# Gate and up of the experts with the hi and lo halves of 64 tokens in one stationary block of 128 columns

## What is computed

```python
def run_block(args):
    tok, g, e = args
    xb = x2[tok]
    hb = jax.nn.silu(xb @ w_gate[e]) * (xb @ w_up[e])
    return (hb @ w_down[e]) * g[:, None].astype(x2.dtype)
```

## Time and profile before

| | |
|---|---|
| median of 3 runs | 2676.31 us (2673.6 to 2676.85) |
| span of the profiled execution | 2682.0 us |
| expert loop, from the first gather to the last subtraction | about 603 to 1222 us |
| PE, DVE, ACT busy over the span | 2241.3, 1577.4, 1063.9 us |
| mean granted clock of TensorE | 0.872 |

### The profile page before, as it was taken

One profiled execution on the slowest core, in us unless ns is written; L12 is line 12 of the kernel. 1 busy time (PEld: TensorE's weight loads), 2 busy tenths in 40 slices (PEclk: granted clock), 3 DMA queues, 4 the chain that ended last, 5 costly groups with the idle time before them and its releaser, 6 DMA issues. The chain is left out here.

```text
span 2682.0 us, 27601 instructions
## 1 busy us (share of the span) xinstructions
PE 2241.3 (84%) x10272; PEld 1841.8 (69%) x10272; DVE 1577.4 (59%) x1629; ACT 1063.9 (40%) x1243; POOL 433.0 (16%) x310
## 2 busy tenths in 40 slices
PE   6998966757999999992897787886488986899997
PEld 5885655656777787772776677765467865688786
DVE  4114578356788788884249999999733244333312
ACT  3224531215677676773243324433343222322211
POOL 0002121001111111110134454343300011000000
PEclk9996557858999999996798988888689998899999
DMA  4210000407999999984232222222023221333321
GB/s 144 73 48 1 1 0 1 167 32 248 324 342 361 333 356 365 357 316 145 51 95 78 64 63 79 79 63 64 0 89 84 94 94 32 87 95 96 107 79 63
DMA packets 251273, 346.55 MB, mean 129 GB/s; under 512 B 13951, under 2 KB 149623, under 8 KB 250151
## 3 DMA queue, kind: packets, MB, share of 16 engines
q1 hardware_dynamic: 240432, 332.49, 37.3%
q0 software_dynamic: 5200, 8.40, 1.0%
q10 hardware_dynamic: 5543, 4.34, 0.5%
HBM read 341.19 MB, written 12.65 MB: 132 GB/s over the span
## 5 line engine op out<-in xcount | busy, mean ns | idle before, releaser
L1335 DVE TENSOR_TENSOR wlo_e<-raw_e,whi_e 128x2048 fp32r<-128x2048 f32 x192 | 432.1, 2292 | 83.6 <-ACT whi_e L1269 83.6
L47 PE MATMUL pall<-hT_hi,w_lo 128*128 128x512 f32 x864 | 354.7, 411 | 53.2 <-DVE yT L2181 33.6
L1646 ACT CAST w_hi<-w_raw 128x2048 fp32r<-128x2048 f32 x89 | 169.5, 1904 | 540.9 <-PE pall L49 540.9
L1654 DVE TENSOR_TENSOR w_lo<-w_raw,w_hi 128x2048 fp32r<-128x2048 f32 x75 | 171.8, 2291 | 352.6 <-ACT w_hi L1646 352.6
L1269 ACT CAST whi_e<-raw_e 128x2048 fp32r<-128x2048 f32 x192 | 357.2, 1914 | 0.0
L48 PE MATMUL pall<-hT_lo,w_hi 128*128 128x512 f32 x864 | 348.1, 403 | 0.0
L49 PE MATMUL pall<-hT_hi,w_hi 128*128 128x512 f32 x864 | 346.5, 401 | 0.0
L2193 DVE SCALAR_TENSOR_TENSOR mixed<-yT,cols,mixed 128x512 f32<-128x512 f32 x240 | 251.2, 1047 | 7.6
L47 PEld LDWEIGHTS pall<-hT_hi,w_lo 128*128 128x128 f32 x864 | 170.4, 197 | 93.5 <-DVE yT L2181 36.4
L47 PE MATMUL pall<-whi_e,xT_lo 128*128 128x512 f32 x512 | 204.6, 400 | 9.6 <-DVE wlo_e L1335 9.6
L49 PE MATMUL pall<-whi_e,xT_hi 128*128 128x512 f32 x512 | 201.2, 393 | 0.0
(11 more groups left out here) (443 smaller groups left out, 4440.0 us busy)
## 6 DMA issues: line engine op xcount, KB each, us to landing
raw_e<-in_w_expert_up_dram SPq DMA_DIRECT2D x64, 1024.0 KB, 8.2
raw_e<-in_w_expert_down_dram SPq DMA_DIRECT2D x64, 1024.0 KB, 7.6
raw_e<-in_w_expert_gate_dram SPq DMA_DIRECT2D x64, 1024.0 KB, 7.1
w_raw<-in_w_in_dram SPq DMA_DIRECT2D x80, 512.0 KB, 5.4
w_raw<-in_w_gate_up_dram SPq DMA_DIRECT2D x44, 512.0 KB, 5.1
w_raw<-in_w_down_dram SPq DMA_DIRECT2D x22, 512.0 KB, 3.9
mixed<-in_w_in_dram SPq DMA_DIRECT2D x10, 1024.0 KB, 5.0
A<-acs_rows SPq DMA_DIRECT2D x8, 1024.0 KB, 4.9
```

The source lines that it names most:

```text
L47: nc.tensor.matmul(out, w_lo, m_hi, start=start, stop=False)
L1335: ins = nc.vector.tensor_tensor(wlo[j][:, :], raw[j][:, :], whi[j][:, :].bitcast(F32), ALU.subtract)
L1646: self.nc.scalar.copy(self.hi[i][:, :], self.raw[i][:, :]).then_inc(self.s_hi, 1)
L1654: (engine or self.nc.vector).tensor_tensor(self.lo[i][:, :], self.raw[i][:, :], self.hi[i][:, :].bitcast(F32), ALU.subtract).then_inc(self ...
```

## The change

Gate and up of one expert take two matmuls per k-block in place of three. The transposed tokens are kept in one tile `xs` of [128, 8, 128], hi of the 64 tokens in columns 0 to 63 and lo in columns 64 to 127. One matmul with all 128 columns stationary and the hi weights moving gives hi x hi in output rows 0 to 63 and lo x hi in rows 64 to 127; a second, with the 64 hi columns stationary and the lo weights moving, adds hi x lo to rows 0 to 63. The two halves are added when the result is turned: `gate_sb` and `up_sb`, copies of the banks in SBUF, are the stationary operands of fp32 matmuls (`combine`) whose moving operand is `st2`, two 64 x 64 identities on top of each other. So silu and the product with up are done in turned form, on 256 columns (`sgT`, `hidT`), and `h_turn` falls away. `y_out` is one copy of 64 x 1024 on ScalarE, one turn later. The loops are unrolled in Python.

```diff
+        xs = sb("xs", [P, KD, 2 * SLOTS], F32R)
+        st2 = sb("st2", [P, SLOTS])
...
             def project(e, out, j0):
                 for j in (j0, j0 + 1):
-                    pe.wait_ge(s["lo"], e * U + j + 1 if not (isinstance(e, int) and e == 0 and j == 3) else U)
+                    pe.wait_ge(s["lo"], made(e, j))
                     for k in range(4):
                         kk = 4 * (j % 2) + k
-                        last = split_mm(nc, out, xT_hi[:, kk, :], xT_lo[:, kk, :], k4(whi[j])[:, k, :], k4(wlo[j])[:, k, :],
-                                        kk == 0, kk == KD - 1)
...
+                        mm(out, xs[:, kk, :], k4(whi[j])[:, k, :], start=kk == 0, stop=False, skip_group_check=True)
+                        last = mm(out[0:SLOTS, :], xs[:, kk, 0:SLOTS], k4(wlo[j])[:, k, :], start=False, stop=kk == KD - 1,
+                                  skip_group_check=True)
...
+            def combine(e):
+
+                pe.wait_ge(s["gate"], e + 1)
+                pe.wait_ge(s["up"], e + 1)
+                if e >= 1:
+                    pe.wait_ge(s["sg"], e)
+                    pe.wait_ge(s["hid"], e)
+                for out, t in ((GT, gate_sb), (UT, up_sb)):
+                    for k in range(4):
+                        last = mm(out[:, k * SLOTS:k * SLOTS + SLOTS], t[:, k * P:k * P + P], st2[:, :], start=True, stop=True)
+                last.then_inc(s["comb"], 1)
...
+            for e in range(E):
+                pe.wait_ge(s["xlo"], e + 1)
+                if e >= 1:
+                    pe.wait_ge(s["gate"], e)
                 project(e, GATE, 0)
-                if not first:
-                    h_turn(e - 1)
+                if e >= 1:
+                    combine(e - 1)
+                    pe.wait_ge(s["up"], e)
                 project(e, UP, 2)
...
+                if e + 1 < E:
+                    x_turn(e + 1)
+                if e >= 1:
+                    down(e - 1)
+            combine(E - 1)
+            down(E - 1)
```

ScalarE's new steps and its order, and VectorE's:

```diff
+            def gate_out(e):
+                act.wait_ge(s["used"], used(e, 1))
+                if e >= 1:
+                    act.wait_ge(s["comb"], e)
+                nc.scalar.copy(gate_sb[:, :], GATE).then_inc(s["gate"], 1)
...
             def silu(e):
-                act.wait_ge(s["used"], e * U + 2)
-                if not isinstance(e, int) or e >= 1:
+                act.wait_ge(s["comb"], e + 1)
+                if e >= 1:
                     act.wait_ge(s["hid"], e)
-                nc.scalar.activation(sg[:, :], GATE, ACT.Silu).then_inc(s["sg"], 1)
+                nc.scalar.activation(sgT[:, :], GT, ACT.Silu).then_inc(s["sg"], 1)
...
+            for e in range(E):
+                hi(e, 3)
+                if e >= 2:
+                    y_out(e - 2)
+                if e >= 1:
+                    hi(e - 1, 4)
+                gate_out(e)
+                if e >= 1:
+                    hi(e - 1, 5)
+                    silu(e - 1)
+                if e + 1 < E:
+                    hi(e + 1, 0)
+                if e >= 1:
+                    h_hi(e - 1)
+                up_out(e)
+                if e + 1 < E:
+                    gathered(e + 1)
+                    hi(e + 1, 1)
+                    hi(e + 1, 2)
...
+            for e in range(E):
+                lo(e, 3)
+                if e >= 1:
+                    lo(e - 1, 4)
+                    lo(e - 1, 5)
+                    hidden(e - 1)
+                if e + 1 < E:
+                    lo(e + 1, 0)
+                if e >= 1:
+                    h_lo(e - 1)
+                if e + 1 < E:
+                    gathered(e + 1)
+                    lo(e + 1, 1)
+                    lo(e + 1, 2)
```

More of the change, by code:

```diff
@@ L1214, in stage_b @@
     g["clear"](s, s_raw, s_mrow)
-    s = {n: sem("e_" + n) for n in "hi lo used xg0 xg xt xhi xlo sg hid ht hhi hlo ya yd ysc".split()}
+    s = {n: sem("e_" + n) for n in "hi lo used xg0 st2 xg xt xhi xlo gate up comb sg hid hhi hlo y ysc".split()}
     s_raw = s_raw_e
@@ L1250, in _ @@
         def _(sp):
[L1251 to L1254, removed]
+            for e in range(1, E):
                 for j in range(U):
-                    sp.wait_ge(s["lo"], e * U - U + j + 1)
-                    load(sp, j, e if j < 4 else e - 1)
+                    at = e if j < 4 else e - 1
+                    if at >= 1:
+                        sp.wait_ge(s["lo"], made(at - 1, j))
+                        load(sp, j, at)
             for j in range(4, U):
-                sp.wait_ge(s["lo"], N_EXPERTS * U - U + j + 1)
-                load(sp, j, N_EXPERTS - 1)
+                sp.wait_ge(s["lo"], made(E - 2, j))
+                load(sp, j, E - 1)
         @block.scalar
@@ L1264, in hi @@
             def hi(e, j):
[L1266 to L1277, removed]
+                act.wait_ge(s_raw[j], 16 * e + 16)
@@ L1298, in turn @@
-            def turn(e, first=False, last=False):
-                hi(e, 3)
-                silu(e)
-                if not first:
[L1302 to L1314, removed]
+                act.wait_ge(s["hid"], e + 1)
@@ L1327, in _ @@
+            y_out(E - 2)
+            silu(E - 1)
+            hi(E - 1, 4)
+            h_hi(E - 1)
+            hi(E - 1, 5)
+            y_out(E - 1)
         @block.vector
@@ L1336, in lo @@
[L1336 to L1343, removed]
+                dve.wait_ge(s["hi"], made(e, j))
@@ L1345, in hidden, with gathered @@
+                nc.vector.tensor_tensor(wlo[j][:, :], raw[j][:, :], whi[j][:, :].bitcast(F32),
+                                        ALU.subtract).then_inc(s["lo"], 3 if (e, j) == (0, 3) else 1)
+            def gathered(e):
+                dve.wait_ge(s["xhi"], e + 1)
+                nc.vector.tensor_tensor(x_lo, turned, x_hi.bitcast(F32), ALU.subtract).then_inc(s["xlo"], 1)
             def hidden(e):
                 dve.wait_ge(s["sg"], e + 1)
-                dve.wait_ge(s["used"], e * U + 4 if not (isinstance(e, int) and e == 0) else 4)
@@ L1358, in y_out @@
[L1358 to L1378, removed]
@@ L1380, in _ @@
-            x_lo(0)
+                nc.vector.tensor_tensor(hT_lo[:, :, :], hidT[:, :].rearrange("p (k t) -> p k t", k=4),
+                                        hT_hi[:, :, :].bitcast(F32), ALU.subtract).then_inc(s["hlo"], 1)
+            gathered(0)
             for j in range(3):
                 lo(0, j)
[L1383 to L1388, removed]
@@ L1393, in _ @@
+            hidden(E - 1)
+            lo(E - 1, 4)
+            h_lo(E - 1)
+            lo(E - 1, 5)
         @block.gpsimd
@@ L1405, in _ @@
             gather(0)
[L1406 to L1417, removed]
+            for e in range(E):
+                pool.wait_ge(s["xt"], e + 1)
+                if e + 1 < E:
+                    gather(e + 1)
+                if e >= 2:
+                    pool.wait_ge(s["y"], e - 1)
+                    scatter(e - 2)
@@ L1419, in _ @@
+            for e in range(E - 2, E):
+                pool.wait_ge(s["y"], e + 1)
+                scatter(e)
+            pool.wait_ge(s["ysc"], 16 * E)
         @block.tensor
         def _(pe):
+            mm = nc.tensor.matmul
             def x_turn(e):
[L1422 to L1426, removed]
-                        w = P if half == k == 0 else turned(e)
-                        last = nc.tensor.transpose(XT[half][:, k * P:k * P + w], xg[0:w, (4 * half + k) * P:(4 * half + k + 1) * P],
-                                                   ident[0:w, 0:w])
-                    last.then_inc(s["xt"], 1)
+                pe.wait_ge(s["xg"], 16 * e + 16)
+                if e >= 1:
+                    pe.wait_ge(s["xlo"], e)
+                for k in range(KD):
+                    w = P if k == 0 else SLOTS
+                    last = nc.tensor.transpose(XT[:, k * SLOTS:k * SLOTS + w], xg[0:w, k * P:k * P + P], ident[0:w, 0:w])
+                last.then_inc(s["xt"], 1)
@@ L1439, in project @@
-                    last.then_inc(s["used"], 3 if isinstance(e, int) and e == 0 and j == 3 else 1)
-            def h_turn(e):
-                pe.wait_ge(s["hid"], e + 1)
-                for k in range(4):
-                    w = P if k == 0 else turned(e)
-                    last = nc.tensor.transpose(HT[:, k * P:k * P + w], hid[0:w, k * P:k * P + P], ident[0:w, 0:w])
-                last.then_inc(s["ht"], 1)
-            def down(e, n):
+                        mm(out, xs[:, kk, :], k4(whi[j])[:, k, :], start=kk == 0, stop=False, skip_group_check=True)
@@ L1450, in down @@
+            def down(e):
                 pe.wait_ge(s["hlo"], e + 1)
[L1451 to L1453 removed]
+                if e >= 1:
+                    pe.wait_ge(s["y"], e)
                 for j in (4, 5):
[L1455 removed]
+                    pe.wait_ge(s["lo"], made(e, j))
                     for half in range(2):
```

104 lines of the change are left out of this document (43 added, 61 removed).

## The result

The changed kernel takes 2731.47 us (median of 4 runs, 2726.23 to 2735.27), the kernel before 2676.58 beside it (2673.6 to 2677.8): a ratio of 1.0204 with a 95% interval of 1.0186 to 1.0221. It is slower by 55 us; the forecast was 2718 us, slower by 42, with 2672 to 2742 as its range. The profiled execution took 2732.13 us, with a span of 2730.3.

A forecast was written before the change was run, and what follows sets the result against it. A ring through TensorE, ScalarE and VectorE was to bind at 18.05 us, with the clock's fall 20.05: 29 turns x (20.05 - 18.67) = +40, +2 at the end, total +42, median 2718 us, range 2672 to 2742.

The forecast's parts named there:

- The bound before: Expert loop of the kernel before: TensorE's own instruction stream binds, 18.1 of 18.32 us in a quiet turn.
- the ring: Changed loop: combine, ScalarE and VectorE steps, down and the next GATE close a cycle of 18.05 us at full clock.
- rival D: Expert loop: loads bound already, turn stays at 18.32 us, only gather waits go; -8 us or nothing, 2668 to 2678; chance 0.04.
- the mis-sized term: Eight fp32 128x64 matmuls adding the halves on TensorE: 0.115 us each, 0.92 us per turn.
- upper bound of 2.8 us: Most that the eight fp32 matmuls could take, from a row of the same shape at half clock, 0.69 us for two.
- The chain: From combine's end through ScalarE and VectorE to down, small steps queued behind weight work: 7.75 us, plus 0.17 us tail.
- the wait at down: TensorE stands still before down, waiting for VectorE's h_lo: about 3.3 us in every turn, nearly 100 us in all.
- The clock: TensorE's granted clock falls to half after the wait in nearly every turn, costing 1.6 to 2.4 us; period taken 20.05 us.
- Outside the steady turns: First two turns held by the first loads as now, 0; after the last turn +2 us (0 to +5).
- rival C: Expert loop: chain hidden, loads bound at 17.1 us per turn from 380 GB/s; -44 us, 2633; chance 0.03.
- Rival A: Expert loop: the clock holds and the ring binds at 18.05 us per turn; -16 us, 2660; chance 0.09.
- point of decision: A chain 0.8 us or more shorter would make TensorE's gaps shorter than any shown to let the clock fall.

The follow-up runs named there:

- f_before_scatter: Kernel before, with each expert's scatter one turn later on GpSimd, so the next gather isn't behind it: 2657.55 us, ratio 0.9911.
- a_fill: Changed kernel plus twelve unread 128x512 matmuls per turn on TensorE between x_turn and down: 2683.42 us, ratio 1.0007.
- b_hlo: Changed kernel with h_lo placed ahead of the next expert's first weight subtraction on VectorE: 2637.37 us, ratio 0.9838.
- c_first: Changed kernel with small steps (silu, h_hi, hidden, h_lo) ahead of the expert's last weight cast and subtraction on ScalarE and VectorE: 2625.9 us, ratio 0.9799.
- h_fill6: Changed kernel plus six unread matmuls per turn on TensorE between x_turn and down: 2683.73 us, ratio 1.0011.
- g_fill3: Changed kernel plus three unread matmuls per turn on TensorE between x_turn and down: 2731.2 us, ratio 1.0187.

## Why the prediction was right, point by point

**The bound before** was TensorE's stream, as said, but not at 18.1 us of work in 18.32: it was 17.885. The 1.2 us put down to x_turn "with the hand-over ahead" held a wait for the gather. The error doesn't touch the forecast, as the ring replaces the stream; it would have spoiled rival D, whose gain of 8 us is 22 in f_before_scatter.

**combine** is the mis-sized term: 0.92 us taken, 1.70 measured. The program has eight fp32 matmuls there and the timeline shows sixteen records. The earlier trace rows were read as 32 matmuls in 3.68 us; the loop at L2407 has 16 for these 32 records (8 x 4 x 4 = 128 in the whole program, 256 records), so the price is 0.23 us each and not 0.115, and eight would have made 1.84. The row was right and the count wrong. As combine lies on the ring, this is nearly all of the 0.84 us per turn between the ring of 18.05 and the 18.89 of a_fill, some 23 us in all. The prediction's own sign, "eight matmuls of combine in 0.9 to 1.1 us", failed with it; its upper bound of 2.8 us for the eight held the 1.70, but the forecast's range had only 0.3 us for the chain and this bound together.

**The chain** of 7.92 us came out as forecast (7.92 with the tail), and so did the wait at down: 3.30 us in the turn shown, 99.9 us for 30. With b_hlo it is shown that this chain, and in it the place of h_lo, is the cause.

**The clock** fell in every turn, as the forecast had it. The price was the lowest of the two worked out, 1.6 us (3.41 us at half clock, all inside down's matmuls), where the middle, 2.0, was taken. That is 0.4 us per turn too much, and it hides half of the error in combine: 18.89 + 1.57 = 20.46 against 18.05 + 2.0 = 20.05. That the total came out so near (55 us for 42) is in this part luck: two errors of opposite sign. The granted clock of the stage was 0.91 and not "about 0.8": 3.41 of 20.46 us at half is 0.92, so the prediction's own 3.2 us would have given it.

**The rest:** the gate copy waits for combine (2.65 us), the DMA share is 0.91, no gather is waited for, ScalarE's casts don't wait for loads; all as listed. Outside the steady turns 0 was taken for the first turns and +2 for the end; the traces have -8 and +6, so both were wrong and nearly cancel. The bound that rival C gave the loads, 17.1 us from 380 GB/s, is what c_first reached, 17.08 at 384. Rival A's mechanism is what a_fill and h_fill6 show by force: with the clock held the result would have been no change, not the 16 us gained, again by the 0.8 us of combine. Its point of decision, "0.8 us or more shorter", was too small a step: at 2.41 us the clock still falls.

## What to carry to other kernels

When work is taken off the busiest engine, find the chain through the other engines that crosses it, and write down what is queued ahead of each small link: here a 0.42-us step behind a 2.29-us one cost 94 us. Put the small steps of a ring ahead of bulk work that has slack, and look for this before judging a change of arithmetic. Count operations in the program and not in the records, and take as the floor of a turn one whose every step between starts is explained.

## What the runs showed of the hardware

A wait of TensorE of 2.41 to 3.30 us behind dense matmuls brought a stretch of 3.41 us at a granted clock of 0.50 in every steady turn of the changed kernel (3.30 us) and in all but one of g_fill3 (2.41 us); one of 1.73 us, behind six more matmuls, brought none in 538 us. But the length of the wait isn't all: with 1.64 us in a turn of 17.23 the clock fell in every eleventh turn, with 1.47 us in one of 20.71 in every eighth. What in these loops decides was not settled. Six or twelve matmuls without use in the wait cost nothing and brought 48 us back.

An fp32 matmul of 128x64 against 128x128 stationary shows as two records and takes 0.21 us in a row at full clock (1.70 us for eight), nearly that of a 128x512 one on the split (fp32r) operands, 0.2275.
